# The v of the next pair turned in the probability banks, and the fillers of the first attention placed over all its steps

## The chip, the cores and the metric

One core of one Trainium2 chip runs the whole program. The metric is the device time of one execution in microseconds, lower is better; three executions of the kernel before were timed, and one more was profiled.

## The reference

Two layers on one sequence of 1024 tokens of width 1024, in fp32. The first one mixes a state-space branch with an attention of 8 heads in which each query keeps its 256 best keys; the second one mixes an attention of 16 heads (three dilated windows, joined by a softmax) with a second state-space branch. Both attentions are what the change touches. Cut to its core, each is:

```python
# first layer: 8 heads share one k and one v; only the chosen keys count
logits = einsum('bqhd,bqkd->bqhk', q, k_sel) * dh ** -0.5
p = softmax(where(valid, logits, -inf));  o = einsum('bqhk,bqkd->bqhd', p, v_sel)
yb = (o * silu(zb)) @ w_b_o
merged = sigmoid(ga) * ya + sigmoid(gb) * yb
x = x + gate * (merged @ w_out)          # gate from c @ w_mod
# second layer, 16 heads with q, k, v and a gate z of their own
q, k, v, z = split(x @ w_in_2)
o = (sum over dilations 1, 4, 16, weighted by a softmax of their log-sums)
y_att = rms_norm(o * silu(z))
```

## The kernel before, in words

Each engine runs its own hand-written instruction stream; semaphores tie them. TensorE does projections as **units**: one unit is one bank of PSUM (128x512), with 24 bf16 matmuls (8 steps of k times three products of a low and a high part, L804) or, for operands that are not split, 8 fp32 passes per half (L801). A unit can be issued in two **halves** of 12 matmuls. Before its first half TensorE waits until the unit that last used the same bank has been evacuated (`bank_before`), and after its last half ScalarE (or, for the gate z, first ScalarE with a tanh and then VectorE at L1887) evacuates it.

Both attentions run `pair_attention`, a pipeline over items: an item is one block of 128 queries for one pair of heads, with i + 1 blocks of 128 keys. The first attention has 32 items, i outermost; the second has 64, eight blocks i = 0 to 7 for each of eight pairs of heads. In step n TensorE does:

1. the scores of item n for its two heads (L857, banks 2 to 5), after VectorE has read the scores of item n - 1;
2. `filler(n, 0)`, a place for half a unit of other work, in bank 0;
3. the transposes of the probabilities of item n - 1 in groups of up to four key blocks (L872, one head in bank 6, the other in bank 7), each group after VectorE has copied the group before it out of the banks; after the first group the weighted sums of the group before (L842, bank 1), and then `filler(n, 1)`, a second place;
4. for i >= 4, the second group of transposes and the weighted sums of the first.

VectorE in step n: scores of item n plus bias with a minimum (L1464, two heads), the copies of the first group of item n - 1 (L1450), the closing product of item n - 2 (L1441, after its weighted sums), the reciprocals of item n (L1475), the copies of the second group, and last `extra(n)`. ScalarE in step n: two exponentials (L1224), place 0 of its evacuations, two scalings by the reciprocal (L1231), place 1 of its evacuations. So an evacuation at place 0 stands before the scalings of the same item, one at place 1 behind them.

**Fillers of the second attention.** While pair j runs, its places compute the ten units of pair j + 1: q, q, k, k, v, v in halves at both places of steps i = 0 to 5; at i = 6 "turned v" 0 at place 0 and the whole unit z 0 at place 1; at i = 7 "turned v" 1 and z 1 likewise. A "turned v" unit is four transposes (L783) of the evacuated v into bank 0, which ScalarE copies back to v's place (L1195). All units of pairs 1 to 7 use bank 0. Pair 0 is computed before this attention, and while the last pair runs there is nothing to fill with.

**Fillers of the first attention.** Sixteen halves of the eight units of gb1 (L804) at place 0 of steps 0 to 15, four halves of gate0 and gate1 (L801) at place 0 of steps 16 to 19, all in bank 0. Steps 20 to 31 have none.

**Queues behind the first attention.** Weights come through two buffers in the order of `LOADS` (... ao, gb1, gate0, gate1, bo, out0 ...), issued by SyncE: load n starts when the last unit of load n - 2 is done, and between loads SyncE stores the evacuated gb1 blocks. GpSimd makes the low parts of a load (`split`, L513, eight instructions) and of each closed block (`gated_low`, L610); `split("bo")` stands after block 19. After block 29 GpSimd issues the transfer of the stored gates gb back (L622, 4 MB, on its own DMA queue), then the last two blocks, two loads of rows, and then, once gb is back, a loop of 16 over the bo units: a product and a sum (L504, L634). The products of out0 on TensorE wait for that loop.

Of the kernel before, what the change touches and what calls it, by code (L numbers as in the profile page):

```python
# [13 lines left out]
P = 128  # L14
# [69 lines left out]
PAIR_UNITS = (("q", 0), ("q", 1), ("k", 0), ("k", 1), ("v", 0), ("v", 1), ("turned v", 0), ("z", 0), ("turned v", 1), ("z", 1))  # L84
BOTH, FIRST_HALF, SECOND_HALF = None, 0, 1
# [8 lines left out]
def unit_plan():  # L94

    count = {"small": 6, "glu": 16, "ao": 16, "bo": 16, "dt": 1, "gate0": 1, "gate1": 1}
    for j in range(8):
        count[f"pair{j}"] = len(PAIR_UNITS)
# [36 lines left out]
CHOSEN = (((30, 0), (4, 0)), ((10, 2), (0, 1)), ((10, 2), (2, 1)), ((6, 3), (2, 1)))  # L135

# [26 lines left out]
def layer_kernel(nc, x, mods, loads, params, consts, rows, alibi, out, x2_dram, gates_dram, q_dram):  # L163
    ctx = ExitStack()
    with ctx:
# [287 lines left out]
        groups1, groups2 = groups_of(items1), groups_of(items2)  # L453
# [41 lines left out]
        def _(pool):  # L495
# [197 lines left out]
            pool.wait_ge(s_att[1]["transposed"], 2 * len(items2) + 2 * 32)  # L693
# [12 lines left out]
        def _(pe):  # L706
            mm = nc.tensor.matmul

            def operands(name, i):
# [35 lines left out]
                if name[:4] == "pair":  # L745
                    what, h = PAIR_UNITS[i]
                    c0 = P * "qkvz".index(what)
                    return KD, [(full, lambda k: weights(KD, k, c0, P), lambda k: acts(hT, k, h * 512, 512))]
# [6 lines left out]
            def unit(u, share=None):  # L755
# [21 lines left out]
                if name[:4] == "pair" and PAIR_UNITS[i][0] == "turned v":  # L777
# [50 lines left out]
            def pair_attention(sems, items, groups, q_of, k_of, v_of, tiles, filler, ready=None):  # L828
# [4 lines left out]
                def weigh(m, g, b0, nb):  # L833
# [6 lines left out]
                    for j in range(nb):  # L840
                        for x in range(2):
                            last = mm(ps[halves[x], 1, 0:P], v_of(items[m], x, b0 + j),  # L842
                                      tiles["cols"][g % 2][x][:, j * P:(j + 1) * P], start=(b0 + j == 0), stop=(b0 + j == i))
                    last.then_inc(sems["weighted"], 1)

                for n in range(len(items) + 1):
# [16 lines left out]
                    if n >= 1:  # L863
                        m = n - 1
                        for g, b0, nb in groups[m]:
# [10 lines left out]
                            pending.append((m, g, b0, nb))  # L876
# [194 lines left out]
            def next_pair(n, place):  # L1071

                j, i = n // 8 + 1, n % 8
                if j < 8 and n < 64:
                    u = FIRST[f"pair{j}"]
                    if i < 6:
                        unit(u + i, place)
                    else:
                        unit(u + 2 * i - 6 + place)

            def pair_ready(n, what):

                j, i = n // 8, n % 8
                if i == 0:
                    pe.wait_ge(s_free, FIRST[f"pair{j}"] + (4 if what == "qk" else 9))
# [5 lines left out]
                           lambda it, x, b: pair_v[it[3] % 2][:, b, DH * x:DH * x + DH], at2, next_pair, pair_ready)  # L1091
# [17 lines left out]
        def _(act):  # L1109
# [8 lines left out]
            def evac(u):  # L1118
# [61 lines left out]
                elif name[:4] == "pair":  # L1180
                    j = int(name[4])
                    what, h = PAIR_UNITS[i]
# [124 lines left out]
            def gate_unit(n, place):  # L1307
                if place:
                    return
                if n == 17:  # L1310
                    for slot in range(2):
                        act.wait_ge(s_spill[slot], 16 * 12)
                if n < 16 and n % 2:
                    evac(FIRST["gb1"] + n // 2)
                elif n in (17, 19):
                    evac(FIRST[f"gate{(n - 17) // 2}"])
# [84 lines left out]
            def next_pair(n, place):  # L1401

                j, i = n // 8 + 1, n % 8
                if j < 8:
                    u = FIRST[f"pair{j}"]
                    if i >= 6:
                        evac(u + 2 * i - 6 + place)
                    elif place == 1:
# [22 lines left out]
        def _(dve):  # L1431
# [11 lines left out]
            def pair_attention(sems, items, groups, tiles, bias_of, close, extra=None):  # L1443

                def copies(g, nb):
                    for x in range(2):
                        dve.wait_ge(sems["transposed"], 2 * g + x + 1)
                        if g >= 2:
                            dve.wait_ge(sems["weighted"], g - 1)
                        V.tensor_copy(tiles["cols"][g % 2][x][:, 0:nb * P], ps[:, 6 + x, 0:nb * P])\  # L1450
                            .then_inc(sems["copied"], 1)

                def closing(m):
                    dve.wait_ge(sems["weighted"], groups[m][-1][0] + 1)
                    close(m, ps[:, 1, 0:P]).then_inc(sems["read"], 1)

                for n in range(len(items) + 1):
# [10 lines left out]
                    if n >= 1:  # L1468
                        copies(*[groups[n - 1][0][q] for q in (0, 2)])
# [6 lines left out]
                    if n >= 1:  # L1476
                        for g, b0, nb in groups[n - 1][1:]:
                            copies(g, nb)
# [403 lines left out]
            def pair_gate_made(j, h):  # L1882

                u = FIRST[f"pair{j}"] + PAIR_UNITS.index(("z", h))
# [32 lines left out]
            def close2(m, o):  # L1917
                j, i = m // 8, m % 8
                if i == 0:
                    dve.wait_ge(s_free, FIRST[f"pair{j}"] + len(PAIR_UNITS))  # L1920
# [151 lines left out]
```

## Time and profile before

| what | us |
|---|---|
| runs, median of 3 (range) | 2242.68 (2241.42 to 2246.37) |
| profiled execution: its time / its span | 2240.73 / 2239.0 |
| TensorE busy over the span | 2025.1 (90%) |
| first attention, from 689 to 873 | 184.0, TensorE busy 168.3 |
| from there to the start of out0 | 68.4 |
| second attention with fillers, from 1538 to 2080 | 542.0, TensorE busy 512.1 |
| its last pair and what follows, from 2080 | 159.0 |

The stages are stretches of the one profiled execution, read from the table of busy time by stretch; times such as "at 1667" are us from the start of its span. Matmuls are pipelined and their ends are modelled, so the start of the next instruction is the better mark of how long TensorE was held.

### The profile page before, as it was taken

The page shows a single profiled execution, that of the slowest core. Times are in us where ns is not written, and L with a number is a line of the kernel's source. Part 1 is how long each engine was busy: PE and PEld are TensorE (multiplying, and loading weights), DVE is VectorE, ACT ScalarE, POOL GpSimd, SP SyncE. Part 2 cuts the span into 40 slices and gives each one's busy share as a digit, 9 for nine tenths or more (in the row PEclk, how much of TensorE's full clock was granted, in tenths as well). Part 3 has the DMA queues.
Part 4 walks back from the last instruction along what each step waited for, and adds up shares of the span by engine and source line. Part 5 has one row for each costly group of instructions (what it writes and reads, how often), then busy time and mean ns, then how long its engine had stood idle before and what let it go on. Part 6 is the DMA issues. An engine that isn't in the chain of part 4 may idle for free.

```text
span 2239.0 us, 27588 instructions
## 1 busy us (share of the span) xinstructions
PE 2025.1 (90%) x10892; PEld 1028.8 (46%) x10892; DVE 1227.9 (55%) x2318; ACT 810.9 (36%) x1358; POOL 620.0 (28%) x638
## 2 busy tenths in 40 slices
PE   3999889988999988696998998999999999999796
PEld 2434335444444555244444665544544444454442
DVE  6428999899992465305454888201433333343516
ACT  3313434433216654113213443312344444334503
POOL 0031416542842022756232224021012012202240
PEclk8999999998999999898999999999999999999998
DMA  7110111211411212213211002011101100110301
GB/s 320 38 47 24 43 38 57 76 65 54 164 38 57 95 38 95 97 54 125 83 38 38 1 1 76 25 51 38 38 1 38 38 14 25 38 39 1 114 19 75
DMA packets 18528, 129.74 MB, mean 58 GB/s; under 512 B 1760, under 2 KB 1760, under 8 KB 13024
## 3 DMA queue, kind: packets, MB, share of 16 engines
q1 hardware_dynamic: 12864, 99.67, 12.0%
q0 software_dynamic: 5536, 28.31, 3.2%
q8 instruction: 86, 1.41, 0.2%
q14 instruction: 42, 0.34, 0.0%
HBM read 109.10 MB, written 18.87 MB: 57 GB/s over the span
## 4 chain that ended last, share of the span: by engine, by line
PE 74%; DVE 15%; ACT 4%; issue 3%; POOL 3%; DMA 2%; SPq 0%; DVEq 0%; POOLq 0%; ACTq 0%
PE ps L804 47%; PE ps L801 7%; PE ps L857 5%; PE ps L842 4%; PE ps L872 3%; DVE arena L1441 3%; POOL arena L504 1%; PE ps L1034 1%; PE ps L1054 1%; DVE small L1611 1%; DVE arena L1599 1%; ACT arena L1224 1%; PE ps L922 1%; POOL arena L634 1%; DVE small L1598 1%
## 5 line engine op out<-in xcount | busy, mean ns | idle before, releaser
L804 PE MATMUL ps<-hT,W 128*128 128x512 bf16 x3456 | 817.7, 391 | 43.8 <-ACT arena L1195 29.7
L804 PEld LDWEIGHTS ps<-hT,W 128*128 128x128 bf16 x3456 | 326.4, 97 | 498.4 <-issue 37.2
L513 POOL TENSOR_TENSOR W<-W 128x512 bf16<-128x512 f32 x224 | 247.7, 1144 | 453.7 <-DMA W<-in_loads 452.5
L804 PE MATMUL ps<-W,arena 128*128 128x512 bf16 x1152 | 262.8, 389 | 20.0 <-DVE arena L1775 19.6
L1450 DVE COPY arena<-ps 128x512 f32<-128x512 f32 (+3 forms) x288 | 147.3, 551 | 238.3 <-PE ps L872 238.0
L1464 DVE CUSTOM_DVE_ANT_0 arena<-ps,arena 128x128 f32<-128x128 f32 (+7 forms) x192 | 138.4, 755 | 202.9 <-PE ps L857 182.8
L1224 ACT ACTIVATE arena<-arena,small 128x128 f32<-128x128 f32 (+7 forms) x192 | 147.4, 768 | 173.6 <-DVE small L1464 173.3
L504 POOL TENSOR_TENSOR arena<-arena 128x512 f32<-128x512 f32 (+1 forms) x80 | 133.3, 1666 | 219.2 <-ACT arena L1376 126.3
L804 PEld LDWEIGHTS ps<-W,arena 128*128 128x128 bf16 x1152 | 111.1, 97 | 170.8 <-DVE arena L1775 20.1
L1231 ACT ACTIVATE arena<-arena,small 128x128 f32<-128x128 f32 (+7 forms) x192 | 138.2, 767 | 116.2 <-DVE small L1475 116.2
L872 PE MATMUL ps<-ck,arena 128*128 128x128 f32 x864 | 124.9, 277 | 25.1 <-DVE arena L1450 19.6
L801 PE MATMUL ps<-arena,W 128*128 128x512 f32 (+1 forms) x320 | 142.0, 598 | 0.9 <-DVE arena L1523 0.9
L804 PE MATMUL ps<-arena,W 128*128 128x512 bf16 x576 | 131.6, 389 | 4.8 <-POOL arena L564 3.8
L673 POOL TENSOR_TENSOR small<-small 128x1024 f32<-128x1024 f32 x7 | 14.0, 1998 | 417.1 <-ACT small L1215 417.1
L872 PEld LDWEIGHTS ps<-ck,arena 128*128 128x128 f32 x864 | 99.1, 140 | 65.4 <-DVE arena L1450 28.1
L842 PE MATMUL ps<-arena 128*64 128x128 f32 x1728 | 127.3, 283 | 0.2
L857 PE MATMUL ps<-arena 64*128 64x512 f32 (+3 forms) x576 | 120.5, 523 | 1.5 <-ACT arena L1201 0.8
L842 PEld LDWEIGHTS ps<-arena 128*64 128x64 f32 x1728 | 92.5, 137 | 24.5 <-issue 23.2
L1611 DVE TENSOR_SCALAR_CACHE_REDUCE small<-arena,small 128x768 bf16<-128x768 f32 (+2 forms) x93 | 101.7, 1143 | 1.1
L804 PE MATMUL ps<-W,hT 128*128 128x512 bf16 (+1 forms) x576 | 94.5, 316 | 4.6 <-issue 2.9
L801 PEld LDWEIGHTS ps<-arena,W 128*128 128x128 f32 (+1 forms) x320 | 57.8, 185 | 78.0 <-issue 75.2
L804 PEld LDWEIGHTS ps<-arena,W 128*128 128x128 bf16 x576 | 55.5, 97 | 80.5 <-POOL arena L564 4.3
(289 smaller groups left out, 2265.4 us busy)
## 6 DMA issues: line engine op xcount, KB each, us to landing
W<-in_loads SPq DMA_DIRECT2D x35, 2048.0 KB, 7.9
gates_scratch<-arena SPq DMA_DIRECT2D x32, 256.0 KB, 2.0
arena<-gates_scratch POOLq DMA_DIRECT2D x2, 4096.0 KB, 13.3
arena<-in_x SPq DMA_DIRECT2D x2, 2048.0 KB, 13.6
W<-in_mods SPq DMA_DIRECT2D x2, 2048.0 KB, 18.3
hT<-in_mods SPq DMA_DIRECT2D x2, 2048.0 KB, 28.8
arena<-in_x POOLq DMA_DIRECT2D x1, 4096.0 KB, 13.7
x_scratch<-arena POOLq DMA_DIRECT2D x8, 512.0 KB, 6.6
```

Of the source, the lines that this page charges most:

```text
L504: return nc.gpsimd.tensor_tensor(o, a, b, ALU.mult)
L513: last = nc.gpsimd.tensor_tensor(low(v), v, high(v), ALU.subtract)
L801: last = mm(o, left, right, start=(k == 0), stop=(k == steps - 1))
L804: last = mm(o, left[:, :, a], right[:, :, b], start=(k == 0 and (a, b) == PRODUCTS[0]), stop=(k == steps - 1 and (a, b) == PRODUCTS[-1]))
L842: last = mm(ps[halves[x], 1, 0:P], v_of(items[m], x, b0 + j), tiles["cols"][g % 2][x][:, j * P:(j + 1) * P], start=(b0 + j == 0), stop=(b0 ...
L857: last = mm(ps[:, 2 + 2 * x + a // BANK, 0:e - a], q_of(items[n], halves[x]), k_of(items[n], halves[x])[:, a:e], start=True, stop=True)
L872: last = nc.tensor.transpose(ps[:, 6 + x, j * P:(j + 1) * P], tiles["rows"][m % 2][x][:, (b0 + j) * P:(b0 + j + 1) * P], ident)
L1224: A(t, t, ACT.Exp, bias=mneg4[:, (n % 2) * 2 + x:(n % 2) * 2 + x + 1], scale=-1.0, accum_out=den[:, (n % 2) * 2 + x:(n % 2) * 2 + x + 1]). ...
L1231: A(t, t, ACT.Copy, scale=rden[:, (n % 2) * 2 + x:(n % 2) * 2 + x + 1]).then_inc(sems["scaled"], 1)
L1450: V.tensor_copy(tiles["cols"][g % 2][x][:, 0:nb * P], ps[:, 6 + x, 0:nb * P])\
L1464: V.tensor_tensor_reduce(tiles["rows"][n % 2][x][:, 0:keys], ps[:, 2 + 2 * x:4 + 2 * x, :].rearrange("p a b -> p (a b)")[:, 0:keys], bias_ ...
L1611: last = V.tensor_scalar(junk[b], sc_at(i), levels[b], None, ALU.is_ge, ALU.add, accum_out=count3[:, b:b + 1])
```

## The change

Four edits. (1) For pairs 1 to 7 the two "turned v" units are gone; instead the group list of the second attention has one more group behind the groups of each item with i = 5 of pairs 0 to 6 (`V_TURNED_AT`), so that the eight transposes of the next pair's v go into banks 6 and 7 behind the last group of that item, in step i = 6, and VectorE copies them to v's place (two copies of 128x512). The group list counts two numbers now: g over all groups (banks 6 and 7), w over those with weighted sums (`cols` buffers, `weighted`). (2) With eight units left, every step i of a pair computes one unit in two halves: z 0 at i = 6, z 1 at i = 7. (3) The halves of gb1, gate0 and gate1 in the first attention go by `GATE_SLOTS`: place 0 of steps 0 to 8, 10, 12 and 14, and place 1 of steps 17, 19, 21, 23 (the last four of gb1), 25, 27 (gate0), 29 and 31 (gate1); ScalarE evacuates in the same place as the second half. (4) `split("bo")` on GpSimd moves from behind block 19 to behind block 26.

```diff
+def pair_units(j):
+    return PAIR_UNITS if j == 0 else [u for u in PAIR_UNITS if u[0] != "turned v"]
...
+GATE_SLOTS = [(n, 0) for n in (0, 1, 2, 3, 4, 5, 6, 7, 8, 10, 12, 14)] + [(n, 1) for n in range(17, 32, 2)]
...
-        def groups_of(items):
-
-            n, out_ = 0, []
-            for it in items:
+        def groups_of(items, with_v=()):
+
+            g, w, out_ = 0, 0, []
+            for n, it in enumerate(items):
                 blocks, mine = it[2] + 1, []
                 for b in range(0, blocks, 4):
-                    mine.append((n, b, min(4, blocks - b)))
-                    n += 1
+                    mine.append((g, w, b, min(4, blocks - b)))
+                    g, w = g + 1, w + 1
+                if n in with_v:
+                    mine.append((g, None, 0, 4))
+                    g += 1
                 out_.append(mine)
...
+        V_TURNED_AT = [8 * j + 5 for j in range(7)]
...
-            for m in range(20):
+            for m in range(27):
                 gated_low(m)
             split("bo")
-            for m in range(20, 30):
+            for m in range(27, 30):
                 gated_low(m)
...
             def gate_unit(n, place):
-                if place == 0 and n < 16:
-                    unit(FIRST["gb1"] + n // 2, n % 2)
-                elif place == 0 and n < 20:
-                    unit(FIRST[f"gate{n // 2 - 8}"], n % 2)
+                if (n, place) in GATE_SLOTS:
+                    q = GATE_SLOTS.index((n, place))
+                    unit(FIRST["gb1"] + q // 2, q % 2)
...
             def next_pair(n, place):
                 j, i = n // 8 + 1, n % 8
                 if j < 8 and n < 64:
                     u = FIRST[f"pair{j}"]
-                    if i < 6:
-                        unit(u + i, place)
-                    else:
-                        unit(u + 2 * i - 6 + place)
+                    unit(u + i, place)
...
+            def turn_v(m, g):
+                j = m // 8 + 1
+                pe.wait_ge(s_free, FIRST[f"pair{j}"] + 6)
+                for x in range(2):
+                    pe.wait_ge(s_att[1]["copied"], 2 * g - 1 + x)
+                    for t in range(4 * x, 4 * x + 4):
+                        last = nc.tensor.transpose(ps[:, 6 + x, (t % 4) * P:(t % 4 + 1) * P],
+                                                   pair_vT[j % 2][:, t * P:(t + 1) * P], ident)
+                    last.then_inc(s_att[1]["transposed"], 1)
...
-                def copies(g, nb):
+                def copies(n, g, w, b0, nb):
                     for x in range(2):
                         dve.wait_ge(sems["transposed"], 2 * g + x + 1)
-                        if g >= 2:
-                            dve.wait_ge(sems["weighted"], g - 1)
-                        V.tensor_copy(tiles["cols"][g % 2][x][:, 0:nb * P], ps[:, 6 + x, 0:nb * P])\
-                            .then_inc(sems["copied"], 1)
+                        if w is None:
+                            to = pair_vT[(n // 8 + 1) % 2][:, x * 512:x * 512 + 512]
+                        else:
+                            to = tiles["cols"][w % 2][x][:, 0:nb * P]
+                            if w >= 2:
+                                dve.wait_ge(sems["weighted"], w - 1)
+                        V.tensor_copy(to, ps[:, 6 + x, 0:nb * P]).then_inc(sems["copied"], 1)
```

On ScalarE `next_pair` evacuates unit i at place 1 of step i, and `gate_unit` the unit whose second half stands at (n, place), gate0's only after the stores of gb1 out of the same memory.

## Rows read from the trace of the kernel before

**Rows 1.** The page: busy time of the engines, and the chain by engine.

```profile
PE 2025.1 (90%) x10892; PEld 1028.8 (46%) x10892; DVE 1227.9 (55%) x2318; ACT 810.9 (36%) x1358; POOL 620.0 (28%) x638
...
PE 74%; DVE 15%; ACT 4%; issue 3%; POOL 3%; DMA 2%; SPq 0%; DVEq 0%; POOLq 0%; ACTq 0%
```

**Rows 2.** Waits, 1538 to 2080 (who <- whom: total, times, longest).

```profile
PE ps L804 <- ACT arena L1195: 29.7, 14, 2.2
```

**Rows 3.** Timeline, steps i = 6 and 7: start us, us, engine, line [idle before].

```profile
1661.49 1.77 PE L857 MATMUL ps<-arena 64*128 64x512 f32 x8
1663.19 0.66 PE L783 MATMUL ps<-ck,arena 128*128 128x128 f32 x4
1663.68 1.04 PE L872 MATMUL ps<-ck,arena 128*128 128x128 f32 x8
...
1664.65 0.44 PE L842 MATMUL ps<-arena 128*64 128x128 f32 x4
...
1667.14 5.62 PE L804 MATMUL ps<-hT,W 128*128 128x512 bf16 x24 [2.05 <-ACT arena L1195]
...
1672.59 0.60 PE L872 MATMUL ps<-ck,arena 128*128 128x128 f32 x4
...
1673.12 1.09 PE L842 MATMUL ps<-arena 128*64 128x128 f32 x16
1673.68 0.68 DVE L1887 SCALAR_TENSOR_TENSOR arena<-arena,ps 128x512 f32<-128x512 f32 x1
...
1674.14 1.99 PE L857 MATMUL ps<-arena 64*128 64x512 f32 x8
...
1676.18 1.22 DVE L1464 CUSTOM_DVE_ANT_0 arena<-ps,arena 128x1024 f32<-128x1024 f32 x1 [1.82 <-PE ps L857]
...
1678.47 1.28 DVE L1450 COPY arena<-ps 128x512 f32<-128x512 f32 x2
...
1679.74 0.57 ACT L1195 ACTIVATE arena<-ps 128x512 f32<-128x512 f32 x1
1679.87 0.16 DVE L1475 RECIPROCAL small<-small 128x2 f32<-128x2 f32 x1
1680.21 2.18 ACT L1231 ACTIVATE arena<-arena,small 128x1024 f32<-128x1024 f32 x2
```

**Rows 4.** Timeline of a half unit in the step that follows.

```profile
1689.61 2.87 PE L804 MATMUL ps<-hT,W 128*128 128x512 bf16 x12
...
1692.32 1.03 PE L872 MATMUL ps<-ck,arena 128*128 128x128 f32 x8
```

**Rows 5.** Busy time by stretch: ends with granted clock, DMA share, GB/s.

```profile
1680.40:1683.60 3.20, 3.20 (x8) 1.14 (x9) 0.00 (x0) 1.99 (x2) 0.00 (x0) 0.50 0.00 0
```

**Rows 6.** The chain in order of time: start us, us, what.

```profile
1746.00 5.62 PE ps L804 x24
...
1823.36 7.19 PE ps L804 x24
```

**Rows 7.** Waits of TensorE, 689 to 873, the first attention.

```profile
PE ps L872 <- DVE arena L1450: 14.6, 19, 1.3
```

**Rows 8.** Timeline, first attention: half of gate0, a step without filler.

```profile
761.71 3.70 PE L801 MATMUL ps<-W,small 128*128 128x512 f32 x8
...
827.34 1.15 PE L872 MATMUL ps<-ck,arena 128*128 128x128 f32 x6 [1.20 <-DVE arena L1450]
```

**Rows 9.** Timeline behind the first attention: GpSimd, and TensorE's first out0 products.

```profile
871.22 0.59 POOL L622 DMA_DIRECT2D arena<-gates_scratch  x1 [0.31 <-POOL arena L610]
...
885.08 1.29 POOL L504 TENSOR_TENSOR arena<-arena 128x512 f32<-128x512 f32 x1 [5.34 <-DMA arena<-gates_scratch]
...
941.37 4.02 PE L804 MATMUL ps<-W,arena 128*128 128x512 bf16 x9 [19.56 <-DVE arena L1775]
```

**Rows 10.** DMA issues (KB each, us to landing), and GB/s by stretch.

```profile
W<-in_loads SPq DMA_DIRECT2D x35, 2048.0 KB, 7.9
...
875.00:880.00 5.00, 4.02 (x43) 2.59 (x42) 1.58 (x3) 0.00 (x0) 1.72 (x4) 1.00 0.97 419
```

More of the change, by code:

```diff
@@ L97, in unit_plan @@
     for j in range(8):
-        count[f"pair{j}"] = len(PAIR_UNITS)
+        count[f"pair{j}"] = len(pair_units(j))
     units, first = [], {}
@@ L776, in unit @@
                     return
-                if name[:4] == "pair" and PAIR_UNITS[i][0] == "turned v":
+                if name == "pair0" and PAIR_UNITS[i][0] == "turned v":
                     h = PAIR_UNITS[i][1]
@@ L826, in turn_tiles, with pair_attention, weigh @@
                         between(n)
-            def pair_attention(sems, items, groups, q_of, k_of, v_of, tiles, filler, ready=None):
+            def pair_attention(sems, items, groups, q_of, k_of, v_of, tiles, filler, ready=None,
+                               turn_v=None):
                 halves = (slice(0, DH), slice(DH, P))
                 pending = []
-                def weigh(m, g, b0, nb):
+                def weigh(m, g, w, b0, nb):
                     i = items[m][2]
@@ L864, in pair_attention @@
                         m = n - 1
-                        for g, b0, nb in groups[m]:
+                        for g, w, b0, nb in groups[m]:
+                            if w is None:
+                                turn_v(m, g)
+                                continue
                             for x in range(2):
@@ L1075, in next_pair @@
                     u = FIRST[f"pair{j}"]
-                    if i < 6:
-                        unit(u + i, place)
-                    else:
-                        unit(u + 2 * i - 6 + place)
+                    unit(u + i, place)
             def pair_ready(n, what):
                 j, i = n // 8, n % 8
-                if i == 0:
-                    pe.wait_ge(s_free, FIRST[f"pair{j}"] + (4 if what == "qk" else 9))
+                if i == 0 and what == "qk":
+                    pe.wait_ge(s_free, FIRST[f"pair{j}"] + 4)
+                elif i == 0 and j == 0:
+                    pe.wait_ge(s_free, FIRST["pair0"] + 9)
+            def turn_v(m, g):
[7 more added lines that the diff above has]
+                    last.then_inc(s_att[1]["transposed"], 1)
             pe.wait_ge(s_free, unit_end("woS1"))
@@ L1307, in gate_unit @@
             def gate_unit(n, place):
[L1308 to L1316, printed above, removed]
+                done = [q // 2 for q in range(1, len(GATE_SLOTS), 2) if GATE_SLOTS[q] == (n, place)]
+                for q in done:
+                    if q == 8:
+                        for slot in range(2):
+                            act.wait_ge(s_spill[slot], 16 * 12)
+                    evac(FIRST["gb1"] + q)
             pair_attention(s_att[0], items1, at1, gate_unit)
@@ L1405, in next_pair @@
                     u = FIRST[f"pair{j}"]
-                    if i >= 6:
-                        evac(u + 2 * i - 6 + place)
-                    elif place == 1:
+                    if place == 1:
                         evac(u + i)
@@ L1468, in pair_attention @@
                     if n >= 1:
-                        copies(*[groups[n - 1][0][q] for q in (0, 2)])
+                        copies(n - 1, *groups[n - 1][0])
                         if n >= 2:
@@ L1476, in pair_attention @@
                     if n >= 1:
-                        for g, b0, nb in groups[n - 1][1:]:
-                            copies(g, nb)
+                        for group in groups[n - 1][1:]:
+                            copies(n - 1, *group)
                     if extra is not None:
@@ L1882, in pair_gate_made @@
             def pair_gate_made(j, h):
-                u = FIRST[f"pair{j}"] + PAIR_UNITS.index(("z", h))
+                u = FIRST[f"pair{j}"] + pair_units(j).index(("z", h))
                 dve.wait_ge(s_tanh, 2 * j + h + 1)
@@ L1919, in close2 @@
                 if i == 0:
-                    dve.wait_ge(s_free, FIRST[f"pair{j}"] + len(PAIR_UNITS))
+                    dve.wait_ge(s_free, unit_end(f"pair{j}"))
                     if j:
```

19 lines of the change are left out of this document (11 added, 8 removed).

## The prediction, made before the changed kernel was built

> **What bounds the kernel now.** I read the page first: TensorE is busy for 90% of the span, and the chain that ended last is TensorE for 74% [rows 1]. So an edit pays where it closes an idle gap of TensorE, or where another engine's chain carries the end. The waits of the two stages that the diff touches come next. In the second attention TensorE has one wait of any size: it stands 29.7 us, in 14 pieces of up to 2.2 us, for ScalarE's L1195, the evacuation of a "turned v" unit [rows 2]; that is two waits for each of the seven pairs whose places are filled. The timeline of one pair shows why. At i = 6 the four transposes of v go into bank 0 at 1663.19, the transposes of the probabilities and a short weighted sum follow, and the whole unit z 0, which needs bank 0 again, starts only at 1667.14 after 2.05 idle [rows 3]. ScalarE takes v out late because its place 0 stands behind both exponentials. At i = 7 the same happens (L1195 at 1679.74) [rows 3]. The first attention loses 14.6 us in 19 waits for L1450, VectorE's copy of the first group, which must leave the banks before the second group enters [rows 7]; by steps, 14.1 of it lies in steps 20 to 31, which have no filler, some 1.2 each [rows 8]. Behind it the end is not TensorE's: gb is issued at 871.22, lands just before 885.08, GpSimd's loop of 16 follows, and out0 starts at 941.37 after 19.56 idle [rows 9]. What counts from the first attention is therefore when gb lands.
>
> **Second attention: the turned v.** Removed: two units with their bank waits and two copies on ScalarE (0.57 each [rows 3]). Added: eight transposes behind the second group of item i = 5. TensorE had these eight already (2 x 0.49, from 1663.19 to 1663.68 [rows 3]), so its work is the same. They wait for the copies of the second group, covered by the weighted sum of the first group that stands between (1.02, 1673.12 to 1674.14 [rows 3]); two copies of 256 columns are under 1.28, the price of two of 512 [rows 3]. The wait for v 1's evacuation is a step old by then. I take 0 for both; 0.5 per pair (3.5 in all) if the cover fails. VectorE gains two copies, 1.28 per pair. Queued behind them on VectorE are the gate product of z 0 (L1887) and the scores of item i = 7.
>
> **Second attention: z in halves.** A half holds TensorE 2.71 (1692.32 - 1689.61 [rows 4]). Step i = 6 put together from [rows 3] and this: scores from 1661.49 for 1.70, half 2.71, first group 0.97, short weighted sum 0.4, half 2.71, second group 0.53, weighted sum 1.02, v 0.98, scores of i = 7 for 1.92: the next half wants bank 0 at 1674.4. VectorE ends its v copies at 1673.3 and, with 0.68 for L1887, frees the bank at 1674.0: 0.4 to spare. For z 1 the chain is longer: the step's scores are in at 1674.4, the copies and the closing product leave the reciprocal at 1679.4; from its start to the end of the scalings it is 2.52 [rows 3], then about 0.6 for the tanh and 0.68 for L1887: free at 1683.3. TensorE wants it (half, first group, 0.6, half, second group 0.75, weighted sum, scores of i = 0) at 1683.6: 0.3 to spare. These are the two thin places. Between 0 and 1.0 us for each of 14 units, I take 0.1, as the sums come out on the near side of zero: 1.4 in all, 14 at the worst. The 29.7 go.
>
> **The clock.** Some z units start at half clock behind their gap: 0.50 granted from 1680.4 to 1683.6, which is 1.2 GHz of 2.4 [rows 5], so a unit takes 7.19 where others take 5.62 [rows 6]. Four of the fourteen z units in the chain are long (7.12 to 7.19; two z 0, two z 1), ten are 5.58 to 5.62: 4 x 1.55 = 6.2 us. Each long one stood right behind a gap of 2 us, and no half unit of steps 0 to 5, which have no gap ahead of them, is long. Without the gaps I take all 6.2 back; the bounds are 0 and 6.2. The Trainium skill ("TensorE: Matmul & The Clock Gate", Part 1) says that the throttled state is the default and activity releases it; these rows agree, as the low level appears only behind idle time.
>
> **First attention.** The halves move from 16 to 21 steps' worth of gaps. Steps 21, 23, 25, 27, 29 and 31 get one at place 1, just where TensorE waits about 1.2 for the copy [rows 8]; a half (2.71, or about 3.6 for gate [rows 8]) is longer than that, so 6.9 of the 14.1 are covered. Uncovered now are steps 9, 11, 13, 15 and 16 (one group; closing product, reciprocal and one scaling against a scores product, some 0.3 each) and step 18 (a gap as in step 20, 1.2), less 0.5 that 17 and 19 had: 2.0, between 0 and 4. TensorE wins 4.9. Other queues: SyncE issues gate1's load after step 23 and needs it at 29; bo's load starts after gate0's last half in step 27 (831, with halves added to and gaps taken from the old step times one by one), lands 7.9 later [rows 10], and GpSimd's split of about 9 ends near 848; it holds back `gated_low` of block 27 by 4, while block 29, which releases gb, closes only at 863. Cover 15 us, price 0. The evacuations move behind the scalings, where ScalarE is idle.
>
> **Where gb lands.** Closing block 29 comes 7.4 sooner (4.9 less the 1.0 of step 31, and a gate half of 3.5 that TensorE now does behind it), so gb is issued at 863.8. But the last half of gate1 also releases SyncE's load of out0 (2 MB), which was long done before and now starts at about 865, in the middle of gb's 4 MB. Alone with the two row loads gb took 13.8 [rows 9]. While gb and rows were in flight together the engines moved 419 GB/s at 0.97 busy [rows 10]: 2.1 MB more is 5.0 us if all of it comes ahead of gb's last packet, 0 if none. So gb lands between 877.6 and 882.6, which is 7.4 to 2.4 sooner than before. I take 3.5, near the full price, since gb is the largest and ends last. The loop and everything behind it shift by that. The tail after 2080 keeps its form.
>
> **Sum.** Against the profiled execution, 2240.7: -29.7 - 6.2 + 1.4 - 3.5 = -38.0, so 2202.7. Its own time is 2.0 below the median of the runs (2242.7); on that scale the forecast is 2204.7.
>
> **Rivals.**
> (a) *The transfers share less than I think, and the first attention brings nothing or costs a little.* For it: a transfer of 2 MB takes 7.9 alone [rows 10], 265 GB/s, and gb 13.8, 304 GB/s [rows 9]; were 304 the ceiling of both together, gb, out0 and rows (7.3 MB) need 24 and gb lands at 888, 3 later than before. Against: 419 in [rows 10]. Time: -29.7 - 6.2 + 1.4 + 3 = -31.5, 2211. The Trainium skill ("DMA: Bandwidth & Descriptors", "Where 436 GB/s comes from") holds that a transfer between HBM and SBUF is bound at about 358 GB/s; by an estimate from that figure gb lands near 886, 1 us late, and the kernel takes 2209. The row with 419 speaks against it, though part of that traffic may be of another kind.
> (b) *The bank is handed on too late.* The wait for L1195 is replaced by one for L1887, which now has the v copies in front of it. With 1.0 for each of 14 units and the clock not regained: -29.7 + 14 - 3.5 = -19, 2223; with half of each, 2213. For it: spare times of 0.3 and 0.4 from sums of ten terms. Against: both come out positive.
> (c) *Slower.* The same place, from the point where L1887 of z 0 ends later than about 1677 in the times of [rows 3], 3 us behind my estimate: 14 waits of 2.8 are 39, more than all gains. It would take VectorE serving the scores of i = 7 ahead of the product, an order that its stream does not have. At 3.5 each the time is 2252.
> (d) *The gaps stay.* The transposes of v stall on the copies as they did on L1195, 2 us once per pair, the clock included: 2225 to 2240.
>
> **Chances.** Forecast with its bounds (2199 to 2209) 0.60, (a) 0.16, (b) 0.14, (d) 0.06, (c) 0.04. The range reaches from everything at its best (29.7 + 6.2 + 7.4 = 43, 2199, with 2 for scatter) to (b) with most of its price, 2197 to 2222. A difference of 0.2%, 4.5 us, is about the least that a measurement of this kernel can tell. Faster takes the forecast, (a), (b) and most of (d): 0.94; same 0.02; slower 0.04.
>
> **What will show it.** In the waits of the second attention L1195 is gone from TensorE, and L1887 stands for under 3 us; the stage from 1538 to 2080 takes about 508 where it took 542, with granted clock 1.00. All z halves take 2.9. In the first attention the waits for L1450 fall from 14.6 to about 9. L622 starts near 864 and lands in 14 to 19; if longer than 21, (a) is right. A step i = 6 longer than 11.2 us between its scores and those of i = 7 points to (b). I am wrong if a wait for `copied` or L1887 appears at i = 6 or 7, or if out0 starts later than 940.

## The result and the profile after

The changed kernel takes 2206.12 us (median of 4, 2203.38 to 2207.63) where the kernel before took 2243.82 beside it (4 runs); the ratio is 0.983, 95% interval 0.9813 to 0.9847. Two more series gave 0.9818 (0.9796 to 0.984) and 0.982 (0.9803 to 0.9837). The forecast was 2204.7. The profiled execution took 2207.47, its span 2205.7, against 2239.0 before: 33.3 less. In the changed file L822 is L804 of before, L894 is L872, L861 is L842, L876 is L857, L1480 is L1450, L1916 is L1887, L1262 is L1231, L640 is L622 (the issue of gb) and L522 is L504 (the first product of GpSimd's loop); L1114 is the transpose of v in its new group. The files of the experiments number the same lines a few off.

The page after, busy time and chain, answers to [rows 1]: TensorE's work is the same to 0.3 us, its share rises from 90% to 92%.

```profile
PE 2024.8 (92%) x10892; PEld 1029.2 (47%) x10892; DVE 1232.5 (56%) x2332; ACT 805.5 (37%) x1344; POOL 618.6 (28%) x638
...
PE 78%; DVE 13%; ACT 3%; POOL 3%; issue 2%; DMA 2%; SPq 0%; DVEq 0%; POOLq 0%; ACTq 0%
```

The waits of the second attention after, 1540 to 2046 (who <- whom: total, times, longest), answer to [rows 2]. TensorE (PE) keeps a single wait for another engine, at the start of the stage. L1916 holds only its weight loads (PEld), which run ahead of the matmuls.

```profile
PEld ps L822 <- DVE arena L1916: 5.3, 7, 0.8
...
PE ps L876 <- ACT arena L1232: 0.8, 1, 0.8
```

The granted clock of the stage is 1.00 (the third figure from the end, as in [rows 5]):

```profile
1540.00:2045.00 505.00, 504.40 (x3169) 262.43 (x3170) 214.29 (x537) 219.08 (x411) 78.27 (x73) 1.00 0.08 30
```

Steps i = 6 and 7 after, from the timeline (start us, us, engine, line), answer to [rows 3]:

```profile
1659.83 1.77 PE L876 MATMUL ps<-arena 64*128 64x512 f32 x8
...
1661.54 2.88 PE L822 MATMUL ps<-hT,W 128*128 128x512 bf16 x12
...
1664.25 1.03 PE L894 MATMUL ps<-ck,arena 128*128 128x128 f32 x8
...
1665.59 2.89 PE L822 MATMUL ps<-hT,W 128*128 128x512 bf16 x12
...
1669.87 1.09 PE L1114 MATMUL ps<-ck,arena 128*128 128x128 f32 x8
1670.57 1.29 DVE L1480 COPY arena<-ps 128x512 f32<-128x512 f32 x2 [1.07 <-PE ps L1114]
1670.90 1.99 PE L876 MATMUL ps<-arena 64*128 64x512 f32 x8
...
1671.77 0.68 DVE L1916 SCALAR_TENSOR_TENSOR arena<-arena,ps 128x512 f32<-128x512 f32 x1
...
1672.82 2.88 PE L822 MATMUL ps<-hT,W 128*128 128x512 bf16 x12
...
1681.27 0.68 DVE L1916 SCALAR_TENSOR_TENSOR arena<-arena,ps 128x512 f32<-128x512 f32 x1
...
1682.10 2.86 PE L822 MATMUL ps<-hT,W 128*128 128x512 bf16 x12
```

From the scores of i = 6 to those of i = 7 it is 11.07 us (1659.83 to 1670.90) where it was 12.65, with no idle time of TensorE between. L1916 ends at 1672.45 and TensorE enters the bank at 1672.82; for z 1 it ends at 1681.95, and the next unit starts at 1682.10. From the first scores of the stage to those of the last pair it is 506.1 us (1540.38 to 2046.47) where it was 542.8 (1537.63 to 2080.38): 36.7 less.

Behind the first attention the picture is another one. GpSimd's timeline and TensorE's first out0 products, which answer to [rows 9]; the line of SPq is SyncE's load of out0:

```profile
867.41 0.59 POOL L640 DMA_DIRECT2D arena<-gates_scratch  x1 [0.31 <-POOL arena L628]
868.45 0.33 SPq L480 DMA_DIRECT2D W<-in_loads  x1
...
885.34 1.28 POOL L522 TENSOR_TENSOR arena<-arena 128x512 f32<-128x512 f32 x1 [7.63 <-DMA arena<-gates_scratch]
...
941.49 4.02 PE L822 MATMUL ps<-W,arena 128*128 128x512 bf16 x9 [21.40 <-DVE arena L1804]
```

gb is issued 3.8 us sooner than before on the clock of the span, and lands 0.3 later: it took 17.8 in place of 13.8. out0 starts 0.1 later. Nothing of the first attention's gain arrives, on the span. Measured from the first filler with an idle mark in front of it (693.69 before, 695.65 after; in the thirteen profiles of this study it stands between 692.3 and 698.1, with no tie to either half of the change), out0 comes after 245.8 in place of 247.7, a gain of 1.8.

The prediction named a start of out0 later than 940 as a sign of being wrong, and 941.49 is later. The issue of gb, forecast at 863.8, came at 867.41, 3.6 later: 2.0 of it lies ahead of the marked filler, and 1.6 is a stretch of low clock in the first attention, which is explained further down. In the other two series out0 started at 939.66 and 938.99.

### The profile page after: what moved, and what is told of

Same layout as the page of the kernel before. It is cut to its first block, busy times and chain, and to the rows that moved or that the text cites. A ratio compares the mean times of both kernels' runs of the same rounds, so it can differ in the third digit from the quotient of the medians.

```text
span 2205.7 us, 27574 instructions
## 1 busy us (share of the span) xinstructions
PE 2024.8 (92%) x10892; PEld 1029.2 (47%) x10892; DVE 1232.5 (56%) x2332; ACT 805.5 (37%) x1344; POOL 618.6 (28%) x638
## 4 chain that ended last, share of the span: by engine, by line
PE 78%; DVE 13%; ACT 3%; POOL 3%; issue 2%; DMA 2%; SPq 0%; DVEq 0%; POOLq 0%; ACTq 0%
PE ps L822 49%; PE ps L819 7%; PE ps L876 5%; PE ps L861 5%; PE ps L894 4%; DVE arena L1467 3%; POOL arena L522 1%; PE ps L1055 1%; PE ps L944 1%; PE ps L1075 1%; POOL arena L652 1%; DMA W<-in_mods 1%; DVE small L1640 1%; DVE arena L1743 1%; DMA arena<-gates_scratch 1%
## 5 line engine op out<-in xcount | busy, mean ns | idle before, releaser
L822 PE MATMUL ps<-hT,W 128*128 128x512 bf16 x3456 | 815.3, 390 | 12.6 <-ACT arena L1174 6.3
L822 PEld LDWEIGHTS ps<-hT,W 128*128 128x128 bf16 x3456 | 324.1, 97 | 466.7 <-issue 34.8
L822 PE MATMUL ps<-W,arena 128*128 128x512 bf16 x1152 | 263.3, 390 | 21.8 <-DVE arena L1804 21.4
L1480 DVE COPY arena<-ps 128x512 f32<-128x512 f32 (+3 forms) x302 | 156.3, 558 | 196.9 <-PE ps L894 189.3
L522 POOL TENSOR_TENSOR arena<-arena 128x512 f32<-128x512 f32 (+1 forms) x80 | 132.6, 1657 | 224.0 <-ACT arena L1404 125.9
L822 PEld LDWEIGHTS ps<-W,arena 128*128 128x128 bf16 x1152 | 111.1, 97 | 173.1 <-DVE arena L1804 21.9
L1262 ACT ACTIVATE arena<-arena,small 128x128 f32<-128x128 f32 (+7 forms) x192 | 138.4, 768 | 126.3 <-DVE small L1504 126.3
L894 PE MATMUL ps<-ck,arena 128*128 128x128 f32 x864 | 124.5, 277 | 20.2 <-DVE arena L1480 13.3
L822 PE MATMUL ps<-arena,W 128*128 128x512 bf16 x576 | 132.6, 391 | 4.7 <-POOL arena L582 3.7
L894 PEld LDWEIGHTS ps<-ck,arena 128*128 128x128 f32 x864 | 100.0, 140 | 64.8 <-DVE arena L1480 18.3
L861 PE MATMUL ps<-arena 128*64 128x128 f32 x1728 | 127.6, 283 | 0.1
L876 PE MATMUL ps<-arena 64*128 64x512 f32 (+3 forms) x576 | 122.2, 530 | 1.5 <-ACT arena L1232 0.8
L861 PEld LDWEIGHTS ps<-arena 128*64 128x64 f32 x1728 | 92.6, 137 | 24.3 <-issue 23.5
L822 PE MATMUL ps<-W,hT 128*128 128x512 bf16 (+1 forms) x576 | 94.9, 316 | 5.7 <-issue 3.9
L822 PEld LDWEIGHTS ps<-arena,W 128*128 128x128 bf16 x576 | 55.9, 97 | 80.9 <-POOL arena L582 4.2
```

Of the source, the lines that this page charges most:

```text
L522: return nc.gpsimd.tensor_tensor(o, a, b, ALU.mult)
L822: last = mm(o, left[:, :, a], right[:, :, b], start=(k == 0 and (a, b) == PRODUCTS[0]), stop=(k == steps - 1 and (a, b) == PRODUCTS[-1]))
L876: last = mm(ps[:, 2 + 2 * x + a // BANK, 0:e - a], q_of(items[n], halves[x]), k_of(items[n], halves[x])[:, a:e], start=True, stop=True)
L894: last = nc.tensor.transpose(ps[:, 6 + x, j * P:(j + 1) * P], tiles["rows"][m % 2][x][:, (b0 + j) * P:(b0 + j + 1) * P], ident)
L1262: A(t, t, ACT.Copy, scale=rden[:, (n % 2) * 2 + x:(n % 2) * 2 + x + 1]).then_inc(sems["scaled"], 1)
L1480: V.tensor_copy(to, ps[:, 6 + x, 0:nb * P]).then_inc(sems["copied"], 1)
```

## The experiments

Each kernel ran beside the kernel before on one chip; ratios are to that. "Filler to out0" is the time from that marked filler to TensorE's first out0 product, "issue" the time from the filler to gb's issue, "gb" its issue to landing, "filled" the second attention from its first scores to those of the last pair; all are from the profiles.

| kernel | ratio (95%) | issue | gb | filler to out0 | filled |
|---|---|---|---|---|---|
| before | 1 | 177.5 | 13.8 | 247.7 | 542.8 |
| changed | 0.983 (0.9813 to 0.9847) | 171.8 | 17.8 | 245.8 | 506.1 |
| changed, second series | 0.9818 (0.9796 to 0.984) | 171.8 | 17.3 | 245.4 | 506.2 |
| changed, third series | 0.982 (0.9803 to 0.9837) | 170.2 | 17.3 | 243.8 | 506.1 |
| second attention only | 0.9844 (0.9827 to 0.9862) | 179.1 | 14.0 | 249.5 | 506.4 |
| first attention only | 0.9979 (0.9968 to 0.999) | 170.1 | 17.5 | 243.9 | 542.7 |
| out0 held | 0.9801 (0.9785 to 0.9817) | 170.2 | 12.6 | 239.1 | 506.2 |
| out0 held, again | 0.9805 (0.9788 to 0.9822) | 170.1 | 12.4 | 239.2 | 506.1 |
| gate early | 0.9814 (0.9796 to 0.9831) | 171.7 | 14.0 | 242.1 | 506.4 |
| before, with the collision | 1.0022 (1.0011 to 1.0032) | 177.5 | 17.7 | 251.5 | 544.5 |
| z whole | 0.9816 (0.9792 to 0.9841) | 171.8 | 17.3 | 245.5 | 506.6 |
| bank handed on 1.4 later | 0.9902 (0.9874 to 0.9929) | 170.1 | 17.2 | 243.6 | 522.1 |
| bank handed on 2.8 later | 1.0059 (1.0038 to 1.0079) | 171.8 | 17.5 | 245.7 | 557.8 |

### Each half of the change alone

The kernel with the edits of the second attention only:

```diff
-                if (n, place) in GATE_SLOTS:
-                    q = GATE_SLOTS.index((n, place))
-                    unit(FIRST["gb1"] + q // 2, q % 2)
+                if place == 0 and n < 16:
+                    unit(FIRST["gb1"] + n // 2, n % 2)
+                elif place == 0 and n < 20:
+                    unit(FIRST[f"gate{n // 2 - 8}"], n % 2)
```

(and the evacuations and the place of the bo split as before).

> Only the edits of the second attention (v turned in banks 6 and 7, z in halves); the first attention's fillers and the place of the bo split are those of before. Theory A (the whole gain is made in the second attention; what the first one wins is taken back by gb's slower transfer): TensorE's waits for L1195 are gone, the stage with fillers takes about 504 us, the kernel takes 2207 to 2210, 34 to 37 us less than before. Rival B (the first attention still brings some 3.5 of the gain, as the sum had it): 2210 to 2213. gb takes 13.8 us in both.

Measured: 2211.52, 0.9844 of before; the filled stage 506.4. The ratio is 35 us of this kernel; the median of before on that chip was 2248.28 with 17 runs from 2240 to 2251, so the absolute time is of less use than the ratio. By the ratio theory A holds (34 to 37 less), by the absolute time alone it would have been rival B. gb took 14.0.

> Only the edits of the first attention (filler slots, place of the bo split); the second attention is that of before. Theory A: gb is issued 4 to 6 us sooner, counted from the first filler, and takes about 18 us, and the kernel takes 2240 to 2244, 0 to 3 us less than before. Rival B: 2236 to 2240, with gb taking 15 or less.

Measured: 2242.42 (12 runs), 0.9979 of before, 4.7 us less (2.2 to 7.2). gb was issued 7.4 us sooner after the marked filler (170.1 for 177.5) and took 17.5: net 3.7. So the first attention does bring a gain, of the size that the sum had (3.5), and theory A was too strict where it expected 0 to 3. The two halves alone, 35.0 and 4.7, add up to 39.7; the three series of the changed kernel are 38.1 to 40.8 below before by their ratios. The waits for the copies of the first group in this kernel, 690 to 880 (they answer to [rows 7], where they were 14.6 in 19), and those that the steps without filler now have for the scalings:

```profile
PE ps L875 <- DVE arena L1449: 8.3, 11, 1.3
PE ps L875 <- ACT arena L1233: 1.7, 5, 0.8
```

6.3 us of waits for copies are gone and 1.5 for scalings have come (1.7 less the 0.2 that the kernel before had). The place of the bo split on GpSimd was not tried by itself. The timeline of the changed kernel has it from 843.47 to 851.5 and then an idle GpSimd before block 29, so it does not hold back gb.

### The two transfers

The cause proposed for gb's longer way is the load of out0. It can be kept off it, in the changed kernel:

```diff
                 if n >= 2:
                     sp.wait_ge(s_unit, unit_end(LOADS[n - 2]))
+                    if LOADS[n] == "out0":
+                        sp.wait_ge(s_back[1], 16)
```

> The changed kernel with one more wait: SyncE issues the load of out0 only after gb is back, so that the two transfers do not overlap. Theory A (the collision cost 4.1 us): gb takes 13.8 us again, the loop behind it starts 4 us sooner, the load of out0 lands long before it is needed, and the kernel takes 2201 to 2203. Rival C (gb is slow for another reason, the rows or the queue of GpSimd): gb stays near 17.9 and the time at 2206.

Measured: 2200.68, 0.9801, as theory A had it. gb takes 12.6, a little less than before the change, and GpSimd's loop starts at once, since the first bo unit is ready at about the same time; its timeline:

```profile
862.41 0.59 POOL L642 DMA_DIRECT2D arena<-gates_scratch  x1 [0.31 <-POOL arena L630]
...
875.08 1.28 POOL L524 TENSOR_TENSOR arena<-arena 128x512 f32<-128x512 f32 x1 [2.39 <-DMA arena<-gates_scratch]
```

The opposite test puts the collision into the kernel before, where nothing else is changed:

```diff
+                    if LOADS[n] == "out0":
+                        sp.wait_ge(s_att[0]["read"], 30)
```

> The kernel before, with one wait more: SyncE issues the load of out0 only when block 29 of the first attention is closed, which is when GpSimd issues gb. It makes the suspected collision by itself, with the fillers where they were. Theory A: gb takes 17.5 to 18 us in place of 13.8, the loop and all behind it start 4 us later, 4 us more than before. Rival C (the slow transfer came from something else in the new order): 13.8 and no change.

Measured: 2252.45 (12 runs), 1.0022 of before, 4.9 us more (2.5 to 7.2). The issue of gb stands where it stood (177.5), gb takes 17.7, out0 comes 3.8 later. Here the load of out0 is issued 0.8 ahead of gb (871.08), in the changed kernel 1.0 behind it (868.45). gb pays about the same in both.

```profile
871.86 0.59 POOL L624 DMA_DIRECT2D arena<-gates_scratch  x1 [0.31 <-POOL arena L612]
...
889.64 1.28 POOL L506 TENSOR_TENSOR arena<-arena 128x512 f32<-128x512 f32 x1 [9.25 <-DMA arena<-gates_scratch]
```

So the collision is both enough and needed: 13.8 becomes 17.7 with it alone, 17.8 becomes 12.6 without it. The load of out0 is slowed too: it takes 18.4 in the changed kernel and 12.7 here, where loads of its size take 7.9 in the median [rows 10]. A third way avoids it by the order of the work, the last eight halves at place 1 of steps 17 to 24:

```diff
-GATE_SLOTS = [(n, 0) for n in (0, 1, 2, 3, 4, 5, 6, 7, 8, 10, 12, 14)] + [(n, 1) for n in range(17, 32, 2)]
+GATE_SLOTS = [(n, 0) for n in (0, 1, 2, 3, 4, 5, 6, 7, 8, 10, 12, 14)] + [(n, 1) for n in (17, 18, 19, 20, 21, 22, 23, 24)]
...
-            for m in range(27):
+            for m in range(24):
```

> The changed kernel with the last eight halves at place 1 of steps 17 to 24 in place of every second step from 17 to 31, and the bo split behind block 23. All gaps up to step 24 are covered, none behind, and out0's load is over before gb starts. Theory A: gb is issued about 2 us later than in the changed kernel (one more half of gate1 stands in front of block 29) or at the same time if the half-clock stretch at step 20 goes, takes 13.8 and lands 2 to 4 us sooner: 2202 to 2204. Rival C: gb takes 17.9 and the time is 2206 to 2208.

Measured: 2203.46, 0.9814; gb takes 14.0 and out0 comes 242.1 after the filler. That is 3.0 later than with the load held: gb is issued 1.5 later, as no half stands behind block 29 any more, and takes 1.4 longer. Why 14.0 and not 12.6: here the loads of the two rows were issued 7.4 us behind gb, with the load held 9.2 us. The profiles agree with that (7.4 and 13.8 in the kernel before, 7.4 and 14.0 with the second attention only, 9.2 and 12.4 in the repeat below), but that this is the cause was not tried.

> The changed kernel with the load of out0 held until gb is back, beside the changed kernel on the same chip. Theory A: 4 to 6 us less than the changed kernel; gb takes 12.6, as before.

> The changed kernel, as the measure for the run with out0 held. Theory A: 0.982 of before, gb takes 17 to 18 us.

Measured on one chip: out0 held 2202.0 (5 runs, 2201.33 to 2203.55), the changed kernel 2205.55 (4 runs, 2205.03 to 2207.4): 3.5 us apart, with no overlap, a little under the 4 to 6 expected. gb took 12.4 and 17.3, and out0 came 4.6 sooner after the filler. It is the best version of this study and beats both kernels. It also shows where the gain of a faster gb ends. GpSimd's loop is released here by ScalarE's evacuation of the first bo unit (L1196), 0.2 behind gb's landing, and no longer by gb:

```profile
877.96 1.28 POOL L524 TENSOR_TENSOR arena<-arena 128x512 f32<-128x512 f32 x1 [2.35 <-ACT arena L1196]
```

### The two edits of the second attention

> The changed kernel once more, on the chip and in the hour of the three that follow, as the measure for them and for the four experiments before. Theory A: its ratio to before lies between that of the kernel with both edits of the second attention alone (0.984) and that with the load of out0 held back (0.980), about 0.982 to 0.983, and gb takes 17 to 18 us. Rival: 0.984, the first attention's edits bring nothing at all.

Measured: 2205.98, 0.9818; gb took 17.3. With it on the same chip, z whole at place 1 and nothing at place 0 of i = 6 and 7:

```diff
                     u = FIRST[f"pair{j}"]
-                    unit(u + i, place)
+                    if i < 6:
+                        unit(u + i, place)
+                    elif place == 1:
+                        unit(u + i)
```

> The changed kernel with z 0 and z 1 issued whole at place 1 of steps i = 6 and 7, place 0 empty, as before; v is turned in banks 6 and 7. It tells the two edits of the second attention apart. Theory D (the wait for L1195 was the whole loss; halves only fill a place that needs no filling): the time of the changed kernel within 2 us, the filled stage takes 505 to 508 us. Rival E (with nothing at place 0 the first group waits for ScalarE's scalings or for the copies, about 1 us per step): 14 us more, the filled stage takes 517 to 522.

Measured: 2206.57 beside 2205.98, the filled stage 506.6 beside 506.2. Theory D holds: halving z does nothing measurable, and the whole loss was that v went through bank 0 and came out behind ScalarE's exponentials. The timeline of step i = 6 in this kernel:

```profile
1658.39 1.09 PE L894 MATMUL ps<-ck,arena 128*128 128x128 f32 x8
1659.41 0.44 PE L861 MATMUL ps<-arena 128*64 128x128 f32 x4
1660.02 5.34 PE L822 MATMUL ps<-hT,W 128*128 128x512 bf16 x23 [0.17 <-issue]
```

### How thin the new place is

The rivals (b) and (c) of the prediction said that the new wait for bank 0 could be late. Idle products on VectorE in front of L1916 (L1920 in these files) make it late; k is 3 or 6:

```diff
+                if j:
+                    idle = ck[:, CONSTS["step"].start:CONSTS["ahead_big"].stop]
+                    for _ in range(k):
+                        link(V.tensor_scalar(idle, idle, 1.0, None, ALU.mult))
                 v = pair_gate(j)[:, h * 512:h * 512 + 512]
```

> The changed kernel with three idle VectorE products of 128x512 (about 0.5 us each, 1.6 in all) in front of each gate product L1916 of pairs 1 to 7. It measures how much time to spare the new wait for bank 0 has. Theory F (0.3 for z 0 and 0.1 to 0.3 for z 1, as the timeline shows): TensorE waits for L1916 14 times, some 1.3 each, 18 us more than the changed kernel. Rival G (more than 1.6 to spare): no change.

Measured: 2223.59, 17.6 more than the changed kernel on that chip; theory F expected 18. An idle product takes 0.43, so three of them put 1.4 us in front of the gate product and six 2.8, not the 1.6 and 3.2 expected. The wait in its profile, 1544 to 2058:

```profile
PE ps L822 <- DVE arena L1920: 17.1, 13, 1.6
```

There are 13 places and not 14, as nothing follows z 1 of the last pair in bank 0. Behind z 0 TensorE waits 1.01 us, which leaves 0.37 of the 1.38 to spare. Behind z 1 the profile has 1.64, but the record of the first matmul is missing there and its weight load starts 0.26 earlier, so 1.4 of it is real: z 1 has next to nothing to spare.

> The same with six idle products, 3.2 us in front of each gate product. Theory F: 14 waits of about 2.9, 41 us more than the changed kernel, so slower than before; and if gaps of TensorE bring the low clock at the start of the next unit, as in the kernel before, some units of 24 or halves of 12 matmuls are long again, up to 1.6 us each. Rival G: 1.6 less for each wait than the added time minus 0.3.

Measured: 2259.27, 1.0059 of before, 53.3 more than the changed kernel: over the 41 of theory F by 12. The wait, 1544 to 2098, and two of the halves behind it, each with the stretch that shows its clock (the last three figures are granted clock, DMA share and GB/s):

```profile
PE ps L822 <- DVE arena L1920: 35.3, 13, 3.2
```

```profile
1681.38 4.49 PE L822 MATMUL ps<-hT,W 128*128 128x512 bf16 x11 [2.39 <-DVE arena L1920]
...
1695.28 4.25 PE L822 MATMUL ps<-hT,W 128*128 128x512 bf16 x11 [3.02 <-DVE arena L1920]
```

```profile
1681.40:1685.70 4.30, 4.24 (x11) 1.61 (x13) 2.21 (x4) 2.39 (x4) 0.00 (x0) 0.60 0.02 6
1695.30:1699.40 4.10, 4.10 (x12) 1.57 (x12) 2.47 (x6) 0.99 (x4) 0.00 (x0) 0.58 0.37 156
```

Halves with 11 recorded matmuls take 2.65 to 2.9 elsewhere in this kernel and 3.9 to 4.5 here. Behind the 13 waits stand eleven such long halves, at some 1.5 each 16 us. 35.3 of waits and 16 of low clock are nearly all of the 51.7 by which its filled stage is longer than that of the changed kernel (557.8 less 506.1). In the kernel with k = 3 no half behind a gap is long, and its granted clock is 1.00 over the stage: the 17.1 of waits, some of them recorded 0.2 too long, explain all of the 16 us there.

## Why the prediction was right, and where it was off

**The turned v: right.** 29.7 us of waits are gone, and nothing waits in their place. "Each half alone" shows it as 35 us of the kernel with the clock, and z whole shows that it is this edit and not the halving that made it.

**The schedule of steps 6 and 7: right to 0.2 us.** The sum had 11.0 from scores to scores and 0.4 and 0.3 us to spare at bank 0. The timeline has 11.07, and the product ends 0.37 and 0.15 before TensorE goes on. The delayed kernels confirm 0.37 at z 0 and put z 1 at next to nothing: 1.4 us more in front of the product gave waits of 1.0 and 1.4. So rival (b) was refuted at z 0 by a reserve that the sum had, and at z 1 by luck as much: by an estimate from these waits, one or two tenths of a microsecond more on VectorE would have made the wait.

**The price of the bank wait: too high.** I took 1.4 for waits in 14 places (there are 13) that came to 0 on TensorE; the loads of weights that do wait (5.3) are hidden by the scores product in front. The filled stage lost 36.7 where I had 34.5: 29.7, 6.2 and 0.8 that I cannot assign. Rival (c) was priced too low for its case: its 2252 counts the 6.2 of the clock as regained in spite of gaps of 3.5 us, and the kernel with six idle products lost another 16 us to the clock.

**The clock: right, and now shown.** All z units run at full clock in the changed kernel, so the 6.2 of [rows 5, 6] came back. That the gaps were the cause was an argument; the kernel with six idle products shows it, as recorded gaps of 2.4 to 3.2 us bring long halves back in 11 of 13 cases and gaps of up to 1.6 in none of 13.

**The first attention: right by its parts, in five profiles of nine.** The issue 7.4 us sooner was measured in five of the nine profiles with the new slots (170.1 to 170.2 for 177.5). In the other four it is 171.8, 5.7 sooner, and the timeline shows why: right behind the gaps of step 20, the scores product of step 21 takes 2.80 to 2.87 where it takes 1.56 in the others, at a granted clock of 0.68 for that stretch. This low clock is not tied to the new slots, for the kernel with the second attention only, which has the old ones, lost 1.6 between filler and issue too, with a clock of 0.91 from 800 to 820. What decides whether it comes was not found.

```profile
781.00:786.00 5.00, 4.73 (x29) 2.69 (x29) 1.50 (x6) 1.96 (x4) 0.40 (x1) 0.68 0.00 0
```

(That is the row of the second series.) The waits for copies fall by 6.3, with the new one of step 18 (0.89) in it, and those for scalings rise by 1.5: 4.8 won where the sum had 4.9. (Its 2.0 for the steps that lose their filler should read 2.2, by its own terms: 1.5 + 1.2 - 0.5.)

**gb's landing: the price right in kind and in size, the time outside its bounds.** The near full price, 3.9 of 5.0, was taken; measured 3.9 (17.7 - 13.8, the landings with and without the collision in the kernel before) and 3.8 to out0 (251.5 - 247.7). Against the held kernel it is 4.9 (17.3 - 12.4). In the profiled changed kernel gb landed at 885.2, outside the 877.6 to 882.6 of the prediction, because it was issued 3.6 later than forecast. What the prediction missed is that the price does not have to be paid: out0's products start 56 us behind gb's landing.

**Rival (a) fell.** While gb and the load of out0 flew together, 426 and 446 GB/s were moved (stretches of the changed kernel, last figure; the third stretch is the kernel with out0 held, with gb alone in flight):

```profile
875.00:879.00 4.00, 3.01 (x20) 1.36 (x17) 0.29 (x1) 0.00 (x0) 1.50 (x3) 1.00 0.99 426
879.00:883.00 4.00, 4.00 (x20) 1.65 (x19) 0.00 (x0) 1.20 (x2) 0.00 (x0) 1.00 1.05 446
867.00:871.00 4.00, 3.42 (x48) 2.67 (x42) 2.09 (x5) 0.00 (x0) 0.49 (x2) 1.00 1.08 467
```

From the issue at 867.41, a ceiling of 304 (24 us for 7.3 MB) would have held gb back until 891, and it landed at 885.2. The prediction left open that part of its 419 was traffic of another kind. It was not: the rates of the stretches from 867.4 to 887 add up to 7.3 MB, which is gb, out0 and the rows. The 358 that the Trainium skill ("DMA: Bandwidth & Descriptors", "Where 436 GB/s comes from") gives for transfers between HBM and SBUF is passed by these rows too; the measurement decides, for a program on one core. (The prediction's estimate from that figure has a slip: 7.3 MB at 358 are 20.5 us, so from 863.8 gb would land at 884 and not at 886.) The same section's 435 for the ports lies between the two stretches of the changed kernel. The 467 of the third, at a busy share of 1.08, lies above it, so rates over 4 us are not exact to better than that.

**The tail: wrong by 0.6 to 2.5.** I wrote that it keeps its form. From the scores of the last pair to the first woA product it is 49.2 us before and with the first attention only (49.5 before with the collision), but 49.8 in the changed kernel and 51.3 to 51.7 in the seven others that have its second attention and no added delay. The work is the same; the low clock comes sooner in that stretch, 0.83 in the kernel with the second attention only (1.00 before) in the first 8 us:

```profile
2050.80:2058.80 8.00, 6.09 (x52) 4.71 (x52) 6.10 (x13) 1.69 (x6) 0.00 (x0) 0.83 0.54 229
```

```profile
2080.40:2088.40 8.00, 6.09 (x66) 4.55 (x66) 6.80 (x18) 2.05 (x7) 0.00 (x0) 1.00 0.55 231
```

(The second row is the kernel before.) The first gap of that pair is 1.91 us in both, so the length of a gap alone does not tell whether the clock falls. In seven of the eight profiles some 2 us of the 36.7 are given back here, where there is nothing to fill with, and 0.6 in the eighth. Why the clock falls sooner behind a stage without gaps is open.

**The sum, and what of it is luck.** On the spans of the two profiles 33.3 stand against 38.0 forecast. The 4.7 between them are: 1.7 less from the first attention (1.8 for 3.5), 2.2 more from the filled stage (36.7 for 34.5), 0.6 in the tail, and 4.6 in stretches that the change does not touch: 2.0 before the first filler, and 2.6 from out0 to the start of the second attention, which begins 2.75 later where out0 began 0.1 later. This last stretch takes 595.7 to 598.9 in the thirteen profiles, with no tie to either half of the change. That the medians of the runs are 37.7 apart, 0.3 from the forecast, is luck in this measure: single stretches scatter by 3 us and more, and an overestimate and an underestimate of 2 us each cancel.

## What to carry to other kernels

When a small step shares a buffer with large ones, look at which engine empties it and what stands in front of that on the engine; moving it to a buffer that another engine already empties in the right place can be worth more than any reordering. When a consumer of a load buffer is moved to a later time, follow the load that it releases: ask what else is then in flight, and hold the one that nobody waits for. And price a gap of the matrix engine with the half-clock stretch that may follow it.

## What the runs showed of the hardware that was not expected

- The 4 MB transfer of gb from GpSimd's queue takes 12.4 to 14.0 us, and 17.2 to 17.8 with 2 MB from SyncE's queue started 1.0 us behind it or 0.8 ahead of it. The 2 MB then take 18.4 and 12.7 in place of 7.9. So neither goes first, and the large transfer pays for nearly all of the small one.
- Gaps of up to 1.64 us as recorded, two for each pair of 75 us of otherwise dense work, left the granted clock at 1.00 (13 gaps). Gaps of 2.04 to 2.19 us were followed by 1.2 GHz in 4 of 14 cases before the change, and gaps of 2.39 to 3.18 in 11 of 13 in the kernel with six idle products. The gap of 1.91 in the last pair was followed by a lower clock in seven of the eight profiles with the new second attention and no delay, and in none of the three with the old one. In the first attention a stretch of low clock also came behind smaller gaps (1.16 and 0.27 us within one step, repeated in every step), in some profiles and not in others.
